# Cache compression of a decoder step, by token rows laid out anew in DRAM and full-fp32 products

## The reference, cut to what matters

```python
NSA_BLOCK, NSA_KV_HEADS, HEAD_DIM, PAGE_SIZE = 64, 2, 128, 128
def compress_kv(kv, pe, w1, w2):                 # kv: B, L, heads, 2 (key, value), 128
    B, L = kv.shape[:2]
    nc = L // NSA_BLOCK
    blk = kv[:, :nc * NSA_BLOCK].reshape(B, nc, NSA_BLOCK, NSA_KV_HEADS, 2, HEAD_DIM)
    blk = blk + pe[None, None, :, None]
    flat = blk.transpose(0, 1, 3, 4, 2, 5).reshape(B, nc, NSA_KV_HEADS, 2, NSA_BLOCK * HEAD_DIM)
    hid = jax.nn.silu(jnp.einsum('bngcf,cfe->bngce', flat, w1))
    return jnp.einsum('bngce,ced->bngcd', hid, w2)

past_cmp = cache_cmp[layer, page_table].reshape(B, past, NSA_KV_HEADS, 2, HEAD_DIM)
ckv = compress_kv(jnp.concatenate([past_cmp, kv_cmp.astype(past_cmp.dtype)], axis=1), pe, w1, w2)
```

## Time and profile before

| what | us |
|---|---|
| device time, median of 3 runs | 2950.51 |
| lowest and highest run | 2947.65 and 2954.24 |
| span of the profiled execution, first to last instruction | 2961.1 |

### The profile page before, as it was taken

The page is one execution under the profiler, slowest core; times in us unless marked ns, Lnnn a source line. Parts: engine busy times, 40 slices in busy tenths (PEclk is TensorE's granted clock), DMA queues, the critical chain, the costliest instruction groups (busy, mean ns, idle before and its releaser), DMA issues.

```text
span 2961.1 us, 55633 instructions
## 1 busy us (share of the span) xinstructions
PE 2816.4 (95%) x22709; PEld 2694.5 (91%) x22709; DVE 2273.6 (77%) x3546; ACT 1391.7 (47%) x2383; POOL 345.4 (12%) x322
## 2 busy tenths in 40 slices
PE   8999999999989878989989999999999999999998
PEld 8999999988878657889989999999999999999997
DVE  6656777877657667755588888888888888888898
ACT  5434455555546544532254444444444454434345
POOL 0010000014270215123320000000000000000002
PEclk9999999999979988999999999999999999999998
DMA  7564443458631883663353435343444464534342
GB/s 221 178 205 110 122 128 109 116 183 283 237 134 52 327 241 107 167 175 87 86 172 112 140 102 141 112 139 107 135 122 130 116 208 155 161 115 145 123 143 99
DMA packets 521999, 440.20 MB, mean 149 GB/s; under 512 B 36270, under 2 KB 476773, under 8 KB 515665
## 3 DMA queue, kind: packets, MB, share of 16 engines
q1 hardware_dynamic: 457906, 303.50, 35.6%
q0 software_dynamic: 19568, 80.16, 7.4%
q10 hardware_dynamic: 44272, 52.98, 5.3%
HBM read 378.33 MB, written 66.55 MB: 150 GB/s over the span
## 4 chain that ended last, share of the span: by engine, by line
PE 49%; DVE 4%; ACT 1%; issue 1%; DMA 1%; POOL 0%; ACTq 0%; POOLq 0%; DVEq 0%
PE i L3373 42%; PE i L140 7%; DVE f_half L3930 1%; DVE x_blocks L3968 1%; DMA x_blocks<-s_blk 0%; DVE h_rows L3963 0%; DMA s_h<-resid 0%; DVE x_blocks L3896 0%; ACT resid L3556 0%; DVE w_ring L3919 0%; ACT x_blocks L3695 0%; DVE ln_parts L3974 0%; PE i L3383 0%; ACT x_blocks L3570 0%; DVE f_sum L3923 0%
## 5 line engine op out<-in xcount | busy, mean ns | idle before, releaser
L3373 PE MATMUL i<-x_blocks,f_half 128*128 128x272 f32 x10752 | 1361.1, 288 | 24.6 <-DVE h_rows L3963 10.7
L3373 PEld LDWEIGHTS i<-x_blocks,f_half 128*128 128x128 f32 x10752 | 1351.4, 189 | 29.9 <-DVE x_blocks L3968 13.9
L570 PE MATMUL a<-xb_in,w_half 128*128 128x272 f32 x4200 | 545.3, 291 | 8.4 <-DVE w_half L972 4.5
L570 PEld LDWEIGHTS a<-xb_in,w_half 128*128 128x128 f32 x4200 | 534.7, 189 | 17.4 <-issue 7.2
L3623 ACT CAST f_half<-w_ring 128x1024 fp32r<-128x1024 f32 (+2 forms) x370 | 346.3, 936 | 403.9 <-PE i L3373 340.4
L3930 DVE TENSOR_TENSOR f_half<-w_ring,f_half 128x1024 fp32r<-128x1024 f32 (+2 forms) x362 | 392.6, 1084 | 81.3 <-ACT f_half L3623 78.9
L3930 DVE TENSOR_TENSOR f_half<-f_sum,f_half 128x1024 fp32r<-128x1024 f32 (+2 forms) x148 | 159.4, 1077 | 80.8 <-ACT f_half L3623 80.6
L972 DVE TENSOR_TENSOR w_half<-w_ring,w_half 128x1024 fp32r<-128x1024 f32 x129 | 157.4, 1221 | 78.6 <-ACT w_half L708 78.3
L3623 ACT CAST f_half<-f_sum 128x1024 fp32r<-128x1024 f32 (+2 forms) x148 | 138.7, 937 | 150.0 <-PE i L3373 150.0
L708 ACT CAST w_half<-w_ring 128x1024 fp32r<-128x1024 f32 x125 | 131.3, 1051 | 109.4 <-PE a L570 105.7
L3336 POOL TENSOR_TENSOR f_half<-w_ring,f_half 128x512 fp32r<-128x512 f32 x8 | 12.6, 1570 | 1400.8 <-ACT f_half L3623 1400.8
(11 more groups left out here) (595 smaller groups left out, 4202.2 us busy)
## 6 DMA issues: line engine op xcount, KB each, us to landing
w_ring<-in_ffn_w_up_dram SPq DMA_DIRECT2D x88, 1024.0 KB
w_ring<-in_w_in_dram SPq DMA_DIRECT2D x52, 1024.0 KB, 8.8
w_ring<-in_ffn_w_down_dram SPq DMA_DIRECT2D x24, 1536.0 KB, 7.6
w_ring<-in_w_o_dram SPq DMA_DIRECT2D x16, 1024.0 KB
x_blocks<-s_blk ACTq DMA_DIRECT2D x17, 816.0 KB, 5.8
s_proj<-st ACTq DMA_DIRECT2D x48, 272.0 KB, 2.7
s_blk<-x_sums ACTq DMA_DIRECT2D x22, 544.0 KB, 6.6
kv_ring<-in_cmp_w_dram SPq DMA_DIRECT2D x16, 512.0 KB, 6.9
```

What stands on the lines that cost most here:

```text
L570: last = nc.tensor.matmul(ps[bank][:, 0:HT2], half(q, w)[:, k], XB[v[j]][:, k], start=j in (0, 1, 3) and k == 0 and i == 0, stop=k == HK - ...
L3373: last = nc.tensor.matmul(ps[bank][:, 0:HT2], half(e, j, wl_)[:, s], XB[:, x0 + s, xl_, BLK_OF[j]], start=start and s == 0 and i == 0, sto ...
```

## The change

A DRAM tensor `S_cmp` with the axes (quarter of the head dimension, token in block, 2 x head + kind, block, 32) takes all blocks: 256 of the past, 8 of the prompt, and two with the position vectors (`NCC` = 266 blocks). SP fills it during the input projection by copies from DRAM to DRAM, whose writes are runs of 32 numbers (128 B): the position vectors in pair 4, seven pages in each pair from 4 on (two copies a page, whose page number SP reads into a register), the prompt's four pages in pair 22.

The compression then has 8 units k = (kind c, half q of the head dimension, head g). A unit loads one tile of token rows, partitions = (quarter h of that half, token), each with 266 blocks x 32 numbers contiguous (three buffers `XC`). For each of its 32 dimensions d PE multiplies a 128 x 128 piece of w1, loaded as it is in 16 pieces (`W1R`), with the 266 columns `XC[:, :, d]`, which lie 32 numbers (128 B) apart, in full fp32, and adds up in one bank for each kind and head: 256 matmuls in all. The product of the position vectors is one of the 266 columns and is added as ACT's bias at the Silu. Transposes, high and low parts, gathers and the prompt's own sums are gone. The keys' product with w2 is issued among the last units. The loads for attention stand later in SP's order: queries after the last row tile, constants after unit 5, keys and values after unit 6.

```diff
+        NCC, DQ = B * NB + SEQ // BLK + 2, HD // 4
+        S_cmp = nc.dram_tensor("s_cmp", (4, BLK, 2 * KVH, NCC, DQ), F32, kind="Internal").ap()
-        def gather(gp, u):
-            gp.indirect_dma_start(XG[:, u % RG], None, pool, bass.IndirectOffsetOnAxis(ap=IDX[:, u % 2, u // 2:u // 2 + 1], axis=0)).then_inc(xg_in[u % RG], 16)
+        NU, NT, NPC = 8, 8, 4
+        XC = [nc.alloc_sbuf_tensor_at(f"token_rows{i}", [P, NCC, DQ], F32, offset=b0 + o) for i, o in enumerate((17408, 78336, 113152))]
+        W1R = [nc.alloc_sbuf_tensor_at(f"w1_{i}", [P, 8, HD], F32, offset=b0 + (60928 if i < 4 else 131072) + 4096 * i) for i in range(2 * NU)]
+        W1v = A["cmp_w1"][0].rearrange("c (t q h d) e -> c q t h d e", q=2, h=2, d=DQ)
+        def rows_load(eng, k, a, b):
+            c, q, g = k // 4, (k // 2) % 2, k % 2
+            eng.dma_start(XC[k % 3][:, a:b], S_cmp[2 * q:2 * q + 2, :, 2 * g + c, a:b].rearrange("h t n e -> (h t) n e")).then_inc(xc_in[k], 16)
+        def w1_load(eng, i):
+            c, q, d0 = i // 8, (i // 4) % 2, (i % 4) * 8
+            for h in range(2):
+                eng.dma_start(W1R[i][h * BLK:(h + 1) * BLK], W1v[c, q, :, h, d0:d0 + 8]).then_inc(w1_in[i], 16)
...
+                def by_token(block, src):
+                    sp.dma_start(S_cmp[:, :, :, block].rearrange("q t k e -> t k q e"),
+                                 src.rearrange("t g c (q e) -> t (g c) q e", q=4)).then_inc(cmp_out, 16)
+                def cached_page(i):
+                    page = nc.sync.value_load(PTS[i // 8:i // 8 + 1, i % 8:i % 8 + 1], min_val=0, max_val=NPOOL - 1)
+                    src = A["cache_cmp_kv"][0, bass.ds(page, 1)]
+                    for n in range(2):
+                        by_token(2 * i + n, src[:, n * BLK:(n + 1) * BLK].rearrange("o t g c d -> (o t) g c d"))
...
+                    if 4 <= e < 23:
+                        for i in range(7 * (e - 4), min(7 * (e - 3), B * NPG)):
+                            cached_page(i)
+                    if e == 22:
+                        for r in range(3):
+                            sp.wait_ge(nat_out[r], 16 * sum(N_NAT[u + 1] for u in range(r, len(KV_UNITS), 3)))
+                        for i in range(QT):
+                            prompt_page(i)
...
-                sp.wait_ge(mq, job(NP_IN - 1, 2) + 1)
-                w1_load(sp, 0)
+                sp.wait_ge(cmp_out, 32 * (B * NPG + QT) + 16 * 4 * KVH)
+                sp.wait_ge(mq, job(NP_IN - 1, 0) + 1)
+                rows_load(sp, 0, 136, NCC)
+                sp.wait_ge(mq, job(NP_IN - 1, 1) + 1)
+                for i in range(4):
+                    w1_load(sp, i)
+                sp.wait_ge(mq, job(NP_IN - 1, 3) + 1)
+                rows_load(sp, 0, 0, 136)
...
+                def rows_again(k):
+                    sp.wait_ge(used, NT * (k - 2))
+                    rows_load(sp, k, 0, NCC)
+                rows_load(sp, 1, 0, NCC)
+                sp.dma_start(W2[:], A["cmp_w2"][0].rearrange("c e d -> e c d")).then_inc(w2_in, 16)
+                for i in (4, 5, 6, 7):
                     w1_load(sp, i)
+                sp.wait_ge(tails_out, 32)
+                rows_load(sp, 2, 0, NCC)
+                for i in (8, 9, 10, 11):
+                    w1_load(sp, i)
+                rows_again(3)
+                rows_again(4)
+                rows_stored(sp)
+                for i in (12, 13, 14, 15):
+                    w1_load(sp, i)
+                rows_again(5)
+                rows_again(6)
+                rows_again(7)
...
+                for u in range(ALL):
+                    k, m = u // NT, u % NT
+                    n, g, c = k // 2, k % 2, k // 4
+                    w = W1R[NPC * n + m // 2]
+                    if g == 0 and m % 2 == 0:
+                        pe.wait_ge(w1_in[NPC * n + m // 2], 32)
+                    if m == 0:
+                        pe.wait_ge(xc_in[k], 32 if k == 0 else 16)
+                    for d in range(4):
+                        last = nc.tensor.matmul(ps[4 + 2 * c + g][:, 0:NCC], w[:, 4 * (m % 2) + d], XC[k % 3][:, :, 4 * m + d],
+                                                start=k % 4 < 2 and m == 0 and d == 0, stop=k % 4 > 1 and m == NT - 1 and d == 3)
                     last.then_inc(used, 1)
+                    if u == ALL // 2 + 13:
+                        keys()
...
+                def hidden(c):
+                    act.wait_ge(pb, c + 1)
+                    for g in range(KVH):
+                        acc = ps[4 + 2 * c + g]
+                        nc.scalar.activation(HID[:, c, g * 256:(g + 1) * 256], acc[:, 0:256], ACT.Silu, bias=PEB[:, c:c + 1])
...
+                def pe_sum(c):
+                    dve.wait_ge(used, (c + 1) * ALL // 2)
+                    nc.vector.tensor_copy(PEB[:, c:c + 1], ps[4 + 2 * c][:, NCC - 2:NCC - 1]).then_inc(pb, 1)
```

More of the change, by code:

```diff
@@ L1174, in build, with at @@
         with ExitStack() as ph:
[L1175 to L1184, removed]
-            HIDX = sb(ph, "hid_heads", [P, KVH, GRP, NPB])
-            PARTS = XP[:, 0, 0:2 * HD].rearrange("p (c d) -> p c d", c=2)
+            def at(name, shape, dt, where):
+                return nc.alloc_sbuf_tensor_at(name, shape, dt, offset=b0 + where)
+            HID = at("hid", [P, 2, B * NB * KVH], F32, 196992)
+            W2 = at("w2", [P, 2, HD], F32, 201088)
+            HIDP = at("hid_p", [P, NPB, KVH], F32, 202112)
+            HIDX = at("hid_heads", [P, KVH, GRP, NPB], F32, 202176)
+            PEB = at("pe_sum", [P, 2], F32, 202432)
             ps = banks(ph, "d")
-            w2_in, xp_in, pr_ps, pr_t, trd, hi, lo, whs, wls, used, acc, accp, hid, out4, ckv = (
-                sem("c_" + n) for n in ("w2_in", "xp_in", "pr_ps", "pr_t", "trd", "hi",
-                                        "lo", "w_hi", "w_lo", "used", "acc", "accp", "hid", "out", "ckv"))
-            pz, pa, pb, pc = (sem("c_" + n) for n in ("parts_zero", "parts", "parts_r", "parts_sum"))
+            ALL = NU * NT
+            w2_in, used, pb, hid, out4, ckv = (
+                sem("c_" + n) for n in ("w2_in", "used", "pe_sum", "hid", "out", "ckv"))
             block = ph.enter_context(nc.Block())
@@ L1291, in _ @@
                         col = g * 256 + b * NB
-                        last = nc.tensor.matmul(ps[(3, 0, 6, 7)[k]][0:NB, u * HD:(u + 1) * HD], HID[:, 1, col:col + NB], W2[:, 1], start=True, stop=True)
+                        last = nc.tensor.matmul(ps[3 + k][0:NB, u * HD:(u + 1) * HD], HID[:, 1, col:col + NB], W2[:, 1], start=True, stop=True)
                     last.then_inc(out4, 1)
@@ L1323, in _ @@
+                hidden(0)
+                hidden(1)
             @block.vector
             def _(dve):
-                def prompt(q):
-                    dve.wait_ge(pr_ps, q + 1)
-                    for c in range(2):
-                        src = ps[6 + q % 2][:, :].rearrange("p (g c n t) -> p c t n g", g=KVH, c=2, n=2)[:, c]
-                        dst = XPT[:, c, :, 4 * q:4 * q + 4].rearrange("p t (n g) -> p t n g", n=2)
-                        for n in range(2):
-                            last = nc.vector.tensor_tensor(dst[:, :, n], src[:, :, n], PET[:, c].rearrange("p (t o) -> p t o", o=1).broadcast_to((P, BLK, KVH)), ALU.add)
-                    last.then_inc(pr_t, 1)
@@ L1355, in _ @@
-                dve.wait_ge(pa, 1)
-                for c in range(2):
-                    last = nc.vector.tensor_copy(PARTS[:, c], ps[6 + c][:, 0:HD])
-                last.then_inc(pb, 1)
-                dve.wait_ge(out4, 1)
+                def pe_sum(c):
+                    dve.wait_ge(used, (c + 1) * ALL // 2)
+                    nc.vector.tensor_copy(PEB[:, c:c + 1], ps[4 + 2 * c][:, NCC - 2:NCC - 1]).then_inc(pb, 1)
+                pe_sum(0)
+                pe_sum(1)
+                dve.wait_ge(out4, 2)
@@ L1470, in _ @@
             def _(pe):
-                pe.wait_ge(kv_in, 144)
+                pe.wait_ge(kv_in, 128)
                 pe.wait_ge(q_in, 16)
```

176 lines of the change are left out of this document (38 added, 138 removed).

## The result

The changed kernel takes 3024.59 us (median of 4 runs, 3022.33 to 3032.81) against 2949.08 us for the kernel before beside it (2946.17 to 2954.24): a ratio of 1.026 [1.0243, 1.0277], 75.5 us more. The forecast was 2911 us. The profiled execution took 3022.33 us with a span of 3020.3.

A forecast was written before the change was run, and what follows sets the result against it. PE was taken as the bound. The stage falls from 174.6 to 127.8 us, gain 46.8; less 2 for loads and 5 for disturbance, 39.8 off gives 2911 us. Own range 2893 to 2928, extended over rival 1, up to 3030.

The forecast's parts named there:

- the pace: Compression's new full-fp32 matmuls: 0.230 us per 266-column instruction, 512 of them taking 117.8 us.
- gain of 39.8: Whole kernel: 46.8 us saved in the compression stage, less 2 for loads and 5 for disturbance.
- The first rival: Compression matmuls: columns 128 B apart stream at half pace, 0.454 us an instruction, total 3024 us; chance 25%.
- The weight loads: Compression on PE: the new matmuls' weight loads fit under the 117.8 us of products.
- Tail: From the compression's last product to attention's first matmul: 8.4 us plus 0.4 us of that product's length, against 13.2 before.
- Loads of the compression: Row tiles and weight pieces, 43.3 MB, arrive just in time for the units; 2 us charged.
- Copying under the projection: Page copies at 0.0129 us a 128 B packet just fit: DMA share 0.95 to 1.01, projection not longer.
- the second rival: Projection: copies above 0.016 us a packet lengthen it, 2957 us mild or 3063 heavy; chances 8% and 10%.
- its other sign: Projection: PE would idle ahead of line 570 behind VectorE's w_half if copying is too dear.
- The disturbance: Full DMA queues delay units and the convolution's small loads (pairs 5 to 7): 5 us, between 0 and 15.
- Third rival, the clock: After the shorter tail the clock may stay up, giving back up to half of 24 us: 2899 us; chance 7%.

The follow-up runs named there:

- the sweep: Changed kernel with each unit reading its moving columns at another step, 4 to 128 B, the last with strided weights, in full fp32: 2988.95 us, single run.
- 7.5 pages a pair: Changed kernel with VectorE copying columns contiguous, page copying begun at pair 6 instead of 4, 7 or 8 pages each: 2935.88 us, ratio 0.9955 to the kernel before.
- 512 B: Changed kernel with its pages copied in runs of 512 B instead of 128 B, products taking other numbers: 3021.43 us, ratio 1.0254 to the kernel before.
- VectorE's copies: Changed kernel with VectorE alone copying the moving columns side by side for all 64 groups of four products: 2922.24 us, run once more 2918.22 us.

## Why the prediction was wrong, point by point

**The failed step** is the pace: "266 columns give 0.225 to 0.232. I take 0.230." The rows it came from the earlier trace rows multiply columns 4 B apart, and for those it was right: contiguous columns run at 0.224 us. At 128 B the instruction takes 0.450 us, so the term 512 x 0.230 = 117.8 us measured 230.4, 112.6 us more. That alone turns a gain of 39.8 into a loss of 72.8. The first rival had exactly this mechanism, place and price (0.454 us an instruction, 3024 us, sign turned above 0.308 us), with a chance of 25%; the range reached over it. How well the price fits is partly luck: it was borrowed from an instruction at half clock, and the sweep shows that "twice" was not given (1.56 times at 12 B, 2.1 at 16 to 124 B). What made me prefer the other was an argument without a row: that two ticks per column leave a reader at half pace enough time. The sweep shows the threshold between 8 and 16 B; the only strided rows of the trace lay at 8 B, on its near side. A free 8 B step said nothing about 128 B.

**The weight loads** "fit under that": right, even with strided weights.

**Tail.** 8.4 + 0.4 us forecast; 9.1 us passed from the last product's start (892.18) to attention's first matmul (901.31). Right.

**Loads of the compression.** 2 us charged, nothing paid at half pace: the window from 661.10 us has no gap. At full pace the charge was too small. In the version with contiguous columns some 11 us went beside the products: 5 us in waits for row tiles ahead of units 2 and 3, which landed 9.4 to 34.2 us after their issue in a queue that they share with the weight pieces, and 6 us at half clock behind standstills. For that half clock the sum had no term; at half pace it cost nothing, since the strided products take 0.450 us at either clock.

**Copying under the projection.** The packet's price was right: 0.0129 us forecast, 0.0112 measured, and the share of 0.95 to 1.01 measured 0.88 to 0.95. PE kept its 22.00 us in both windows of the earlier trace rows. That it "just fits" was right too, with nothing to spare: SP's wait for w_half is gone (0.9 us in 330 to 600), and at 7.5 pages a pair w_in's tiles come late. That wait alone was thus no sign of the second rival; its other sign, PE idle ahead of the projection's products, did not come, and neither did the rival. (Its sum has a slip: 25.3 us a pair are 3.3 over 22, not 3.1, so 2960 us and not 2957. The text also counts 54 tiles and 27 pairs in the projection; the code has 52 and 25, of some 22.5 us each. Neither changes the forecast.)

**The disturbance**, 5 us forecast: the copying alone measured 6.7 us in the kernel before. In the profiled execution of the changed kernel the compression began 12.95 us later: 10.6 us in the projection and 2.3 in a longer wait for the barrier behind it (5.60 us on PE's sequencer, 3.27 before). The place was right, the small loads for the convolution, and so was the size within its bounds. PE waits 5.2 us for them in 204:244, against 2.2 before; a further loss follows from the granted clock, 0.91 in 204:244 against 1.00 before, with 24 matmuls in 5.67 us instead of 3.29. Counted by its matmuls, the projection of the changed kernel was 7.5 us behind by pair 8, held that, and lost 3.1 more in the last pairs. Such a late loss came in some profiled executions (5.5 us with contiguous columns) and not in others (none with 512 B or VectorE's copies), and its cause stays open.

**Third rival, the clock.** Behind the shorter tail it was granted 0.59 in the stretch where the earlier trace rows show 0.50, and 0.65 and 0.64 in the two executions with VectorE's copies. That is far from staying up. Attention and what follows took 2119.0 us in the changed kernel's trace and 2138.4 in the trace of before, but 2124.8 in the kernel before with copying, whose compression is the old one. Most of that difference is therefore the profiled execution of before, which was 10.6 us above its median.

**The sum again**, with what was measured: -39.8 + 112.6 (pace) - 2 (loads) + 0.3 (tail) + 8 (start of the stage, 12.95 instead of 5) = +79.1 us, against 78.6 in the traces up to attention and 75.5 in the medians. The spans of the two profiled executions differ by less, 59.2 us, for the reason just given.

## What to carry to other kernels

Before a layout saves work, price how TensorE reads it: a moving operand whose fp32 columns lie 16 B or more apart takes twice as long in full fp32, and a row measured at 8 B says nothing about it. If the layout is wanted anyway and VectorE is idle, one strided copy per group of products, shorter than the products it feeds, buys the pace back; here that turned +75.5 us into -28 and -31 us. Large copies hidden under a bound engine are not free even where they fit: look at the share in the few microseconds in which small loads are due, not at the mean of the stage.

## What was not expected of the hardware

- A step of 8 B costs full fp32 almost nothing (0.235 against 0.224 us for 266 columns) and halves the pace of fp32r (0.238 against 0.126 us).
- 12 B lies between (0.350 us), and 128 B (0.450 us) is a little better than 16, 32 and 124 B (0.470 to 0.479 us).
- Strided columns keep their pace when the clock halves: at 128 B 0.450 us at a granted clock of 0.50 and of 1.00, where contiguous ones take 0.446 and 0.224.
- ScalarE needs 2.04 us for a copy of 1,064 numbers per partition at a step of 128 B, VectorE 1.21 us.
- Weights with columns 128 B apart load in 298 ns (full fp32, hidden) and 320 ns (fp32r, not hidden: 0.225 instead of 0.124 us an instruction), against 189 ns contiguous.
- From DRAM to DRAM a packet of 512 B takes 2.4 times as long as one of 128 B (0.0271 against 0.0112 us), so a byte in runs of 128 B is 1.65 times as dear. The Trainium skill (DMA: Bandwidth & Descriptors, Specifications) names a read-modify-write below 512 B; the rows show the dearer byte, but not what it comes from.
